# Centring the values inside the RWKV-7 recurrence, and splitting the squares of its output into a rounded and a low part

## The chip, the cores and the metric

One core of one Trainium2 chip runs the whole program in one launch. The time is device microseconds (us) from launch to end, the median of several executions; lower is better. Engine names in the profile: PE is TensorE's matmul, PEld its weight load, DVE is VectorE, ACT is ScalarE, POOL is GpSimd, SP is SyncE, which issues most transfers.

## The reference, cut to what matters

The model is two layers of a block with three branches (RWKV-7, retention, a spatial gating unit), each followed by a gated feed-forward part, and then a second block with attention and experts. The change lies in the RWKV-7 branch, whose output is normalised per head of 64 features:

```python
def rwkv7_scan(r, w, k, v, kk, a):
    def step(state, inp):
        sa = jnp.einsum('bhvk,bhk->bhv', state, -kk_t)
        state = (state * w_t[:, :, None, :] + sa[..., None] * (kk_t * a_t)[:, :, None, :]
                 + v_t[..., None] * k_t[:, :, None, :])
        y = jnp.einsum('bhvk,bhk->bhv', state, r_t)
        return state, y
...
y = rwkv7_scan(r, decay, k, v, kk, a)                       # (1, 512, 8, 64)
mean = jnp.mean(y, axis=-1, keepdims=True)
var = jnp.mean(jnp.square(y - mean), axis=-1, keepdims=True)
y = (y - mean) * lax.rsqrt(var + RW_GN_EPS) * lnx_g + lnx_b
y = y + jnp.sum(r * k * r_k, axis=-1, keepdims=True) * v
```

The output y is linear in v, and the feature index over which the mean is taken is v's own. A v from which the mean over its 64 features was taken therefore gives a y whose mean over them is zero. The bonus term at the end uses v itself, uncentred.

## The kernel before

Activations lie with features on the 128 partitions and 512 tokens along the row: a 1024 wide activation is eight tiles of 128x512, the RWKV-7 output y four (`PAIRS`, two heads of 64 in a tile). Large products are made in three passes: the weights and the activations are split into a rounded part in the type fp32r and a low part (what rounding left), and hi·hi, hi·lo and lo·hi are added up in one PSUM bank. The weights' rounded part is made by ACT (`high`, L1309) and their low part by POOL (`low`, L1437); the low part of an activation is made by DVE. Products whose operands are plain f32 are not split; the trace shows two PE instructions for each of those.

`back_phase` runs once for each of the two layers. Its first part is 24 tiles, i = 0 to 23 (`gate_and_branch(i)`): a gate product of depth 8 (L1485, L1489, L1494), then a branch product of depth 4 (L1505, L1514, L1520), for the retention branch in tiles 0 to 7, the gating unit in 8 to 15 and RWKV-7 in 16 to 23. Between the passes of tiles 0 to 10, `beneath(slot)` places the recurrence itself: chunks of 64 tokens, worked on by small 64x64 f32 matmuls (L960, L1075, L1087). Each engine has its own program, written out by hand in the order of issue, and the engines wait for each other on semaphores that count up.

What the change touches, by engine:

- PE. In three of the recurrence's turns (`TURNS`, through `by_features`, L956 to L960) beta, value and kappa are turned from features-by-tokens to tokens-by-features by a matmul against the identity. Behind tile 10, `means()` (L1525 to L1529) sums y over each head with four matmuls against a block matrix of ones (`head_ones`); behind tile 11, `variances()` (L1531) does the same for the squares; behind tile 12, `out_gates()` (L1541) makes four more products.
- DVE. `recurrence_vector` (L1200) begins with a copy of the chunks' decay (L1203). It is issued behind `begin_x` (L990) and `low_y(RET, 0)` (L1774, four subtractions), and ahead of the first mask (L1242), which empties the PSUM bank that PE's next slot writes to. `centre()` (L1777, its instruction is L1780) subtracts the mean from y behind tile 10, in place.
- ACT. In tile 11, behind the gate's sigmoid, `squares()` (L1665) squares the centred y into `sq`; `logs()` and `roots()` turn the variances into factors.
- POOL. `low(n)` for the gate and the branch of each tile, 128x1024 and 128x512, and one mask of the recurrence (`next_bt`, L996) for each level.

In each tile POOL's `low` follows ACT's `high`, and ACT's follows the last pass of PE's product before.

Of the kernel before, what the change touches and what calls it, by code (L numbers as in the profile page):

```python
# [17 lines left out]
F32 = mybir.dt.float32  # L18
F32R = mybir.dt.float32r
ALU = mybir.AluOpType  # L20
# [3 lines left out]
P = 128  # L24
# [882 lines left out]
class Recurrence:  # L907
# [4 lines left out]
    def __init__(self, nc, T, home, R):  # L912
        U = self.U
        in_x = iter(range(KD))
        in_w = iter(range(6))
        in_runs = iter((60, 62, 64, 66))

        def x(_):
            return T.xT[:, next(in_x), :].rearrange("p (u c) -> p u c", u=U)

        def w(_):
            i = next(in_w)
            return T.w[:, 0, i * S:i * S + S].rearrange("p (u c) -> p u c", u=U)

        def runs(n):
            return over(nc, home + next(in_runs) * 1024, "rec_" + n, U, C)

        self.LT, self.X, self.T1, self.BT = x("LT"), x("X"), x("T1"), x("BT")
        self.bT, self.kT, self.vT = (x("bT0"), w("bT1")), (x("kT0"), w("kT1")), (x("vT0"), w("vT1"))
        self.XT, self.AkT = (x("XT0"), runs("XT1")), (w("AkT0"), runs("AkT1"))  # L930
        self.AbrT, self.AkrT = (w("AbrT0"), runs("AbrT1")), (w("AkrT0"), runs("AkrT1"))
        self.M, self.Rs, self.Un = (over(nc, home + kb * 1024, "rec_" + n, PAIRS, C)
                                    for kb, n in ((69, "M"), (48, "Rs"), (49, "Un")))
        self.decay = over(nc, home + 68 * 1024 + 512, "rec_decay", PAIRS, NCH)
        self.masks, self.alpha, self.beta, self.rho, self.kappa = R.masks, R.alpha, R.beta, R.rho, R.kappa
        self.value, self.y = R.p[:, 8:12, :], R.y

# [18 lines left out]
def by_features(nc, T, Q, g, bank, lhs, rhs, u, h):  # L956

    half, j, now = HEAD_HALVES[h], u % PAIRS, chunk_tokens(2 * g + u // PAIRS)
    rhs = T.ident[half, half] if rhs is None else rhs[half, j, now]
    return nc.tensor.matmul(bank[token_half(h), u * C:u * C + C], lhs[half, j, now], rhs, start=True, stop=True)  # L960


# [36 lines left out]
def recurrence_tensor(nc, T, pe, q, Q):  # L999
# [19 lines left out]
    def wait_fill(g, t):  # L1019
        if t == KEY_SUM:  # L1020
            pe.wait_ge(q["lt_ready"], g + 1)
        elif t == BETA_TURN:
            pe.wait_ge(q["masked"], 3 * g + 1)
        elif t == BETA_SUM:
            pe.wait_ge(q["turned_taken"], 3 * g + 1)
        elif t == VALUE_TURN:
            pe.wait_ge(q["masked"], 3 * g + 2)
        elif t == KAPPA_TURN:
            pe.wait_ge(q["turned_taken"], 3 * g + 2)
        elif t == KAPPA_SUM:  # L1030
            pe.wait_ge(q["turned_taken"], 3 * g + 3)
        elif t == NEXT_L:
            pe.wait_ge(q["masked"], 3 * g + 3)
# [166 lines left out]
def recurrence_vector(nc, T, dve, q, Q, R):  # L1200

    link = Chain(dve, q["clock"])
    link(nc.vector.tensor_copy(Q.decay[:, :, :], R.runs[:, :, :, C:C + 1].rearrange("p j n a -> p j (n a)")))  # L1203

    def change_state(n):
        dve.wait_ge(q["change_done"], n + 1)
# [10 lines left out]
    def beneath(slot):  # L1217
# [34 lines left out]
        if changing:  # L1252
# [3 lines left out]

REC_SEMS = ("operands_ready product turned turned_taken t1_done t1_taken lt_ready bt_ready masked x_ready xt_begun xt_ready "
            "step_done zeroed right_begun change_begun right_done right_taken y_begun u_done u_taken y_part change_done "
            "changed state_ready y_done y_taken clock")


BACK_SEMS = ("m_full*2 x_full w_full*2 w_hi w_lo done clock loaded mean_done centred squared var_done rooted gate_done out_done "
             "y_hi y_lo sig_done added m_hi m_lo x_added x_squared sq_added x_summed norm_rooted "
             "sg_gated u_hi u_lo scaled taps_loaded gate_taken val_taken conv_done silu_done made gains_made z_hi z_lo")
BACK_ORDER = (1, 2, 0)
# [74 lines left out]
class BackWork:  # L1340


    def __init__(self, nc, T, home):
        def at(skip, name, *shape, dt=F32):
            return over(nc, home + int(skip * 1024), "back_" + name, *shape, dt=dt)

        self.y_hi = (at(16, "y_hi_ret", 4, S, dt=F32R), at(106, "y_hi_sg", 4, S, dt=F32R),
                     at(52, "y_hi_rw", 4, S, dt=F32R))
        self.y_lo = (at(0, "y_lo_ret", 4, S, dt=F32R), at(8, "y_lo_sg", 4, S, dt=F32R),
                     at(40, "y_lo_rw", 4, S, dt=F32R))  # L1350
        self.merged, self.m_lo = at(86, "merged", KD, S), at(86, "m_lo", KD, S, dt=F32R)
        self.sq, self.rstd, self.up = at(24, "sq", PAIRS, S), at(32, "rstd", PAIRS, S), at(70, "up", RW_W)
        self.w_hi, self.w_lo = T.next_hi, T.w_lo
        self.m_hi, self.sig = at(0, "m_hi", KD, S, dt=F32R), at(102, "sig", 2, S)

        self.made_hi, self.made_lo = at(0, "made_hi", FT, S, dt=F32R), at(44, "made_lo", FT, S, dt=F32R)
        self.sq_sum, self.x_rstd = at(102, "sq_sum", S), at(104, "x_rstd", S)
        self.un, self.x_sq = at(106, "un", 4, S), at(106, "x_sq", 2, S)
        self.conv, self.taps = at(88, "conv", 4, S), at(132, "taps", FT, 8)
        self.next_sq = at(106, "next_sq", 2, S)  # L1360


def back_phase(nc, T, f, q, stale, layer, R, y_ret, y_sg, B, Q, late, gain):
# [33 lines left out]
    with nc.Block() as block:  # L1397
# [59 lines left out]
        def _(pe):  # L1457
# [64 lines left out]
                mm.then_inc(f["done"], 1)  # L1522
                beneath(next(slots))

            def means():  # L1525
                pe.wait_ge(q["y_taken"], NCH)
                for j in range(PAIRS):
                    nc.tensor.matmul(T.ps[4 + j][:, :], T.head_ones[:, :], y_rw[:, j, :], start=True,
                                     stop=True).then_inc(f["mean_done"], 1)  # L1529

            def variances():  # L1531
                for j in range(PAIRS):
                    pe.wait_ge(f["squared"], j + 1)
                    nc.tensor.matmul(T.ps[4 + j][:, :], T.head_ones[:, :], B.sq[:, j, :], start=True,
                                     stop=True).then_inc(f["var_done"], 1)

            def out_gates():
# [80 lines left out]

            for i in range(24):
                gate_and_branch(i)  # L1620
                if i == 10:
                    means()
                if i == 11:
                    variances()
                if i == 12:
                    out_gates()
# [20 lines left out]
        def _(act):  # L1647
# [12 lines left out]
                    nc.scalar.copy(B.y_hi[part][:, k, :], y[part][:, k, :]).then_inc(f["y_hi"], 1)  # L1660

            def squares():
                for j in range(PAIRS):
                    act.wait_ge(f["centred"], j + 1)
                    nc.scalar.activation(B.sq[:, j, :], y_rw[:, j, :], ACT.Square).then_inc(f["squared"], 1)  # L1665

            def logs():

# [99 lines left out]
        def _(dve):  # L1768
# [5 lines left out]
                    nc.vector.tensor_tensor(B.y_lo[part][:, k, :], y[part][:, k, :], B.y_hi[part][:, k, :].bitcast(F32),  # L1774
                                            ALU.subtract).then_inc(f["y_lo"], 1)

            def centre():  # L1777
                for j in range(PAIRS):
                    dve.wait_ge(f["mean_done"], j + 1)
                    nc.vector.scalar_tensor_tensor(out=y_rw[:, j, :], in0=T.ps[4 + j][:, :], scalar=-1.0 / 64,  # L1780
                                                   in1=y_rw[:, j, :], op0=ALU.mult, op1=ALU.add).then_inc(
                                                       f["centred"], 1)

            def finish_out(j):

# [81 lines left out]
            for i in range(24):  # L1867
# [6 lines left out]
                if i == 5:  # L1874
                    low_y(SG, 4)
                if i == 10:
                    centre()
                if i in (13, 14):
                    finish_out(2 * i - 26)
                    finish_out(2 * i - 25)  # L1880
# [2085 lines left out]
```

## Time and profile before

| what | value |
|---|---|
| median of 3 runs (lowest to highest) | 2836.72 us (2835.44 to 2837.39) |
| span of the profiled execution, first to last instruction | 2839.8 us |
| PE busy | 2777.4 us, 98% |
| DVE, ACT, POOL busy | 1445.8, 1099.1, 1080.0 us: 51%, 39%, 38% |
| granted TensorE clock, mean | 0.994 |
| transfers | 413.83 MB, 146 GB/s on average |

The profile is one execution, and its span is 3.1 us (0.1%) longer than the median of the runs; the runs themselves lie within 2 us. A busy share says little of a single stretch. In a stretch where PE has no gap, what leaves PE shortens the program, and what leaves another engine doesn't. Where PE has a gap, the question is what ended it. In the views, times are from the start of the span; the last bracket of a timeline row is the idle time ahead of it and the instruction that released it. The first layer's back phase starts at about 254 us, the second's at about 1176 us.

### The profile page before, as it was taken

What the parts mean: (1) busy time and instruction counts of PE and PEld (TensorE: products, weight loads), DVE (VectorE), ACT (ScalarE), POOL (GpSimd) and SP (SyncE); (2) the same over time, 40 slices, a digit from 0 to 9 for tenths busy, and PEclk for the clock granted to TensorE, in tenths of its full rate; (3) what the DMA queues carried; (4) which work ended last, traced back from release to release, by engine and by line L of the source; (5) the groups of instructions that cost most, each with busy time, mean ns of one, the idle gap of its engine ahead of it and who ended that gap; (6) DMA issues with size and microseconds to landing.
All of it is one profiled execution on the core that took longest, in us unless ns stands there. A gap on an engine that the chain in (4) does not pass through costs nothing. (4 is left out here: it accounts for less than half of the span.)

```text
span 2839.8 us, 45477 instructions
## 1 busy us (share of the span) xinstructions
PE 2777.4 (98%) x18996; PEld 2064.6 (73%) x18997; DVE 1445.8 (51%) x1776; ACT 1099.1 (39%) x1613; POOL 1080.0 (38%) x627
## 2 busy tenths in 40 slices
PE   8999999999999999999999999999999989999997
PEld 6777777888888877777888888877778764445543
DVE  6267434578862526743457785269855232222223
ACT  4484324343332448433434333255575331111112
POOL 4365433444444436543444444434444221211110
PEclk9999999999999999999999999999999999999999
DMA  5222122222222422212222232232222149999995
GB/s 178 75 86 72 48 106 89 83 92 102 94 107 96 164 71 86 72 48 106 89 87 100 89 104 96 97 107 84 88 79 104 48 189 387 419 414 413 411 411 235
DMA packets 63070, 413.83 MB, mean 146 GB/s; under 512 B 9504, under 2 KB 10272, under 8 KB 25632
## 3 DMA queue, kind: packets, MB, share of 16 engines
q1 hardware_dynamic: 62880, 411.11, 38.4%
q8 instruction: 142, 2.33, 0.3%
q14 instruction: 48, 0.39, 0.0%
HBM read 401.64 MB, written 4.19 MB: 143 GB/s over the span
## 5 line engine op out<-in xcount | busy, mean ns | idle before, releaser
L1437 POOL TENSOR_TENSOR w_lo<-w,next_hi 128x1024 fp32r<-128x1024 f32 (+1 forms) x244 | 546.3, 2243 | 644.9 <-ACT next_hi L1656 433.9
L1656 ACT CAST next_hi<-w 128x1024 fp32r<-128x1024 f32 (+1 forms) x152 | 156.0, 1026 | 268.7 <-PE bank L1468 249.3
L312 POOL TENSOR_TENSOR w_lo<-w,next_hi 128x1024 fp32r<-128x1024 f32 x64 | 162.3, 2537 | 223.5 <-ACT next_hi L510 223.5
L3506 PE MATMUL bank<-moe_w,moe_hg 128*64 128x512 f32 x1024 | 225.8, 594 | 0.0
L2291 POOL TENSOR_TENSOR mid_w_lo<-w,mid_w_hi 128x1024 fp32r<-128x1024 f32 x60 | 149.2, 2490 | 183.8 <-ACT mid_w_hi L2753 183.4
L3506 PEld LDWEIGHTS bank<-moe_w,moe_hg 128*64 128x64 f32 x1024 | 73.4, 137 | 141.1 <-issue 141.1
L1463 PE MATMUL bank<-h_hi,next_hi 128*128 128x512 f32 x688 | 171.1, 391 | 1.5 <-DVE back_made_lo L1861 1.5
L1465 PE MATMUL bank<-h_lo,next_hi 128*128 128x512 f32 x688 | 169.9, 389 | 0.0
L1468 PE MATMUL bank<-h_hi,w_lo 128*128 128x512 f32 x688 | 169.9, 389 | 0.0
L1748 ACT ACTIVATE back_conv<-back_un,back_taps 128x512 f32<-128x512 f32 x88 | 71.8, 816 | 238.8 <-DVE back_un L1845 238.8
L1309 ACT CAST next_hi<-w 128x1024 fp32r<-128x1024 f32 x96 | 80.1, 835 | 213.3 <-PE bank L1494 157.4
L1463 PEld LDWEIGHTS bank<-h_hi,next_hi 128*128 128x128 f32 x688 | 129.0, 188 | 29.9 <-DVE back_made_lo L1861 2.3
L1465 PEld LDWEIGHTS bank<-h_lo,next_hi 128*128 128x128 f32 x688 | 129.2, 188 | 26.8
L1468 PEld LDWEIGHTS bank<-h_hi,w_lo 128*128 128x128 f32 x688 | 129.2, 188 | 26.8
L1849 DVE SCALAR_TENSOR_TENSOR back_conv<-back_un,back_taps,back_conv 128x511 f32<-128x511 f32 x88 | 90.2, 1026 | 86.6 <-ACT back_conv L1748 86.6
L3447 POOL COPY moe_quad_place<-moe_place 128x16 f32 (+1 forms) x7 | 1.4, 198 | 347.7 <-PE bank L3560 347.7
L510 ACT CAST next_hi<-w 128x1024 fp32r<-128x1024 f32 x64 | 66.9, 1045 | 130.0 <-PE bank L392 69.0
L3574 PE MATMUL bank<-moe_w,moe_midT 128*64 128x512 f32 x512 | 113.3, 595 | 2.6 <-ACT moe_midT L3650 2.6
L1860 DVE CAST back_made_hi<-back_conv 128x512 fp32r<-128x512 f32 x44 | 109.6, 2491 | 1.5
L1827 DVE TENSOR_TENSOR xT<-xT,bank 128x512 f32<-128x512 f32 x32 | 22.0, 688 | 172.1 <-PE bank L1468 170.1
L1812 DVE TENSOR_TENSOR back_sig<-back_sig,bank 128x512 f32<-128x512 f32 x32 | 22.0, 688 | 171.0 <-PE bank L1520 131.7
L3697 DVE TENSOR_TENSOR xT<-xT,bank 128x512 f32<-128x512 f32 x120 | 74.3, 681 | 65.0 <-PE bank L3520 65.0
(620 smaller groups left out, 6478.4 us busy)
## 6 DMA issues: line engine op xcount, KB each, us to landing
moe_w<-in_moe_w SPq DMA_DIRECT2D x128, 1024.0 KB, 13.1
moe_w<-in_moe_w SPq DMA_DIRECT2D x32, 2048.0 KB, 12.3
w<-in_ffn_up SPq DMA_DIRECT2D x44, 1024.0 KB, 4.8
w<-in_w_merge SPq DMA_DIRECT2D x48, 768.0 KB, 4.3
w<-in_w_in SPq DMA_DIRECT2D x30, 1024.0 KB, 4.9
w<-in_w_mid SPq DMA_DIRECT2D x29, 1024.0 KB, 4.8
w<-in_ffn_down SPq DMA_DIRECT2D x16, 1408.0 KB, 5.8
w<-in_w_out SPq DMA_DIRECT2D x16, 512.0 KB, 4.4
```

Of the source, the lines that this page charges most:

```text
L312: nc.gpsimd.tensor_tensor(split(w_lo, c, t), raw(c, t), split(w_hi, c, t).bitcast(F32), ALU.subtract).then_inc(f["w_lo"], 1)
L1309: nc.scalar.copy(w_hi[:, n % 2, 0:merge_depth(n), :], merge_raw(T, n)).then_inc(f["w_hi"], 1)
L1437: nc.gpsimd.tensor_tensor(split(B.w_lo, n), raw(n), split(B.w_hi, n).bitcast(F32), ALU.subtract).then_inc(f["w_lo"], 1)
L1463: nc.tensor.matmul(bank, B.w_hi[:, n % 2, k, :], x_hi[:, cols], start=start and k == 0, stop=False)
L1465: nc.tensor.matmul(bank, B.w_hi[:, n % 2, k, :], x_lo[:, cols], start=False, stop=False)
L1468: mm = nc.tensor.matmul(bank, B.w_lo[:, n % 2, k, :], x_hi[:, cols], start=False, stop=stop and k == len(hi) - 1)
L1656: nc.scalar.copy(split(B.w_hi, n), raw(n)).then_inc(f["w_hi"], 1)
L1849: link(nc.vector.scalar_tensor_tensor(out=c[:, 1:S], in0=u[:, 0:S - 1], scalar=tap(1), in1=c[:, 1:S], op0=ALU.mult, op1=ALU.add))
L1860: link(nc.vector.tensor_copy(hi, product))
L2291: nc.gpsimd.tensor_tensor(split(B.w_lo, n), raw(n), split(B.w_hi, n).bitcast(F32), ALU.subtract).then_inc(f["w_lo"], 1)
L3506: mm = nc.tensor.matmul(bank[half_of(u), :], hg[:, k, slots_of(b, u)], w[:, u, k * 512:k * 512 + 512], start=(k == 0), stop=(k == KD - 1))
L3574: mm = nc.tensor.matmul(y_banks[half][half_of(u), :], midT[:, f, half_of(u)], w2[:, u, c:c + 512], start=(f == 0), stop=(f == 3))
```

## The change

Three edits, in each of the two layers.

1. The recurrence gets values that are already centred. A 64x64 matrix, the identity less 1/64 everywhere (`Q.centre`, once for each half of the partitions), is made by two DVE instructions at the start of the recurrence and takes the identity's place when the values are turned. PE waits for the two (semaphore `centre_made`) ahead of that turn.
2. `means()` on PE and `centre()` on DVE go, with their semaphores.
3. ACT rounds the ones to fp32r (`sum_heads`) and squares y straight into an fp32r tile (`sq_hi`). DVE makes the whole squares in f32 (`sq`) and subtracts the rounded ones (`sq_lo`). The sum over a head is one fp32r product of the rounded part and one of the low part, where there was one f32 product.

```diff
 def by_features(nc, T, Q, g, bank, lhs, rhs, u, h):
-    rhs = T.ident[half, half] if rhs is None else rhs[half, j, now]
+    if rhs is None:
+        rhs = Q.centre[half, :] if lhs is Q.value else T.ident[half, half]
+    else:
+        rhs = rhs[half, j, now]
...
         elif t == VALUE_TURN:
+            pe.wait_ge(q["centre_made"], 2)
             pe.wait_ge(q["masked"], 3 * g + 2)
...
     link(nc.vector.tensor_copy(Q.decay[:, :, :], ...))
+    for half in HEAD_HALVES:
+        nc.vector.scalar_tensor_tensor(out=Q.centre[half, :], in0=T.head_ones[half, half], scalar=-1.0 / C,
+                                       in1=T.ident[half, half], op0=ALU.mult, op1=ALU.add).then_inc(q["centre_made"], 1)
...
-            def means():
-                pe.wait_ge(q["y_taken"], NCH)
-                for j in range(PAIRS):
-                    nc.tensor.matmul(T.ps[4 + j][:, :], T.head_ones[:, :], y_rw[:, j, :], start=True,
-                                     stop=True).then_inc(f["mean_done"], 1)
-
             def variances():
                 for j in range(PAIRS):
                     pe.wait_ge(f["squared"], j + 1)
-                    nc.tensor.matmul(T.ps[4 + j][:, :], T.head_ones[:, :], B.sq[:, j, :], start=True,
+                    nc.tensor.matmul(T.ps[4 + j][:, :], B.sum_heads[:, :], B.sq_hi[:, j, :], start=True, stop=False)
+                    pe.wait_ge(f["sq_split"], j + 1)
+                    nc.tensor.matmul(T.ps[4 + j][:, :], B.sum_heads[:, :], B.sq_lo[:, j, :], start=False,
                                      stop=True).then_inc(f["var_done"], 1)
...
             def squares():
+                act.wait_ge(q["y_taken"], NCH)
+                nc.scalar.copy(B.sum_heads[:, :], T.head_ones[:, :])
                 for j in range(PAIRS):
-                    act.wait_ge(f["centred"], j + 1)
-                    nc.scalar.activation(B.sq[:, j, :], y_rw[:, j, :], ACT.Square).then_inc(f["squared"], 1)
+                    nc.scalar.activation(B.sq_hi[:, j, :], y_rw[:, j, :], ACT.Square).then_inc(f["squared"], 1)
...
-            def centre():
+            def split_squares():
+
+                dve.wait_ge(q["y_taken"], NCH)
                 for j in range(PAIRS):
-                    dve.wait_ge(f["mean_done"], j + 1)
-                    nc.vector.scalar_tensor_tensor(out=y_rw[:, j, :], in0=T.ps[4 + j][:, :], scalar=-1.0 / 64,
-                                                   in1=y_rw[:, j, :], op0=ALU.mult, op1=ALU.add).then_inc(
-                                                       f["centred"], 1)
+                    nc.vector.tensor_tensor(B.sq[:, j, :], y_rw[:, j, :], y_rw[:, j, :], ALU.mult).then_inc(
+                        f["sq_whole"], 1)
+                for j in range(PAIRS):
+                    dve.wait_ge(f["sq_whole"], j + 1)
+                    dve.wait_ge(f["squared"], j + 1)
+                    nc.vector.tensor_tensor(B.sq_lo[:, j, :], B.sq[:, j, :], B.sq_hi[:, j, :].bitcast(F32),
+                                            ALU.subtract).then_inc(f["sq_split"], 1)
```

DVE at the start of the first layer's recurrence, before. `back_y_lo_ret` is the low part of the retention branch's output, `w` the tile that the first mask fills:

```order
118 L1774 TENSOR_TENSOR back_y_lo_ret_215<-y_ret,back_y_hi_ret_209 128x512 x4
119 L1203 COPY rec_decay_267<-rw_runs 128x32
120 L1242 TENSOR_TENSOR w<-bank,rw_masks_207 128x512
121 L1810 TENSOR_TENSOR back_merged_221<-back_sig_233,bank 128x512
122 L1226 TENSOR_TENSOR xT<-xT,bank 128x512
```

The same place in the changed program:

```order
119 L1208 COPY rec_decay_273<-rw_runs 128x32
120 L1210 SCALAR_TENSOR_TENSOR rec_centre_275<-head_ones,ident 64x64 x2
121 L1250 TENSOR_TENSOR w<-bank,rw_masks_207 128x512
122 L1820 TENSOR_TENSOR back_merged_221<-back_sig_239,bank 128x512
123 L1234 TENSOR_TENSOR xT<-xT,bank 128x512
```

Two instructions now stand between the copy of the decay and the first mask; both read two tiles in SBUF.

PE at the ends of tiles 10 and 11, before (the 64x64 work is over by then):

```order
1644 L1520 MATMUL bank<-back_y_hi_sg_211,w_lo_57 128x512 x4
1645 L1528 MATMUL bank<-rw_p,head_ones 128x512 x4
1646 L1485 MATMUL bank<-h_hi_50,next_hi_55 128x512 x8
1647 L1489 MATMUL bank<-h_lo,next_hi_55 128x512 x8
1648 L1494 MATMUL bank<-h_hi_50,w_lo_57 128x512 x8
1649 L1505 MATMUL bank<-back_y_hi_sg_211,next_hi_55 128x512 x4
1650 L1514 MATMUL bank<-back_y_lo_sg_217,next_hi_55 128x512 x4
1651 L1520 MATMUL bank<-back_y_hi_sg_211,w_lo_57 128x512 x4
1652 L1534 MATMUL bank<-back_sq_225,head_ones 128x512 x4
1653 L1485 MATMUL bank<-h_hi_50,next_hi_55 128x512 x8
```

And in the changed program, from the end of tile 11:

```order
1650 L1530 MATMUL bank<-back_y_hi_sg_211,w_lo_57 128x512 x4
1651 L1538 MATMUL bank<-back_sq_hi_225,back_sum_heads_229 128x512
1652 L1540 MATMUL bank<-back_sq_lo_227,back_sum_heads_229 128x512
1653 L1538 MATMUL bank<-back_sq_hi_225,back_sum_heads_229 128x512
1654 L1540 MATMUL bank<-back_sq_lo_227,back_sum_heads_229 128x512
1655 L1538 MATMUL bank<-back_sq_hi_225,back_sum_heads_229 128x512
1656 L1540 MATMUL bank<-back_sq_lo_227,back_sum_heads_229 128x512
1657 L1538 MATMUL bank<-back_sq_hi_225,back_sum_heads_229 128x512
1658 L1540 MATMUL bank<-back_sq_lo_227,back_sum_heads_229 128x512
1659 L1495 MATMUL bank<-h_hi_50,next_hi_55 128x512 x8
```

The four f32 products against the ones (L1528) are gone from the end of tile 10, and the four of tile 11 have become eight in fp32r, each of the low ones behind a wait of its own.

DVE at the same tiles, before and then in the changed program:

```order
210 L1812 TENSOR_TENSOR back_sig_233<-back_sig_233,bank 128x512
211 L1817 TENSOR_TENSOR back_merged_221<-back_merged_221,back_sig_233 128x512
212 L1780 SCALAR_TENSOR_TENSOR rw_p<-bank,rw_p 128x512 x4
213 L1812 TENSOR_TENSOR back_sig_233<-back_sig_233,bank 128x512
214 L1817 TENSOR_TENSOR back_merged_221<-back_merged_221,back_sig_233 128x512
```

```order
211 L1822 TENSOR_TENSOR back_sig_239<-back_sig_239,bank 128x512
212 L1827 TENSOR_TENSOR back_merged_221<-back_merged_221,back_sig_239 128x512
213 L1786 TENSOR_TENSOR back_sq_231<-rw_p 128x512 x4
214 L1791 TENSOR_TENSOR back_sq_lo_227<-back_sq_231,back_sq_hi_225 128x512 x4
215 L1822 TENSOR_TENSOR back_sig_239<-back_sig_239,bank 128x512
216 L1827 TENSOR_TENSOR back_merged_221<-back_merged_221,back_sig_239 128x512
```

Four instructions with one input in PSUM have become eight that read SBUF alone, and tile 11's addition to the merged tile stands behind them.

## Rows read from the trace of the kernel before

**Rows 1.** The page: busy us of each engine, share of the span, instructions
```profile
PE 2777.4 (98%) x18996; PEld 2064.6 (73%) x18997; DVE 1445.8 (51%) x1776; ACT 1099.1 (39%) x1613; POOL 1080.0 (38%) x627
```
**Rows 2.** Timeline of PE, tiles 10 to 12: start, us, instructions
```profile
414.17 3.59 PE L1528 MATMUL bank<-rw_p,head_ones 128*128 128x512 f32 x8
417.19 2.39 PE L1485 MATMUL bank<-h_hi,next_hi 128*128 128x512 f32 x8
419.42 1.98 PE L1489 MATMUL bank<-h_lo,next_hi 128*128 128x512 f32 x8
421.24 1.98 PE L1494 MATMUL bank<-h_hi,w_lo 128*128 128x512 f32 x8
...
425.77 3.59 PE L1534 MATMUL bank<-back_sq,head_ones 128*128 128x512 f32 x8
428.80 2.39 PE L1485 MATMUL bank<-h_hi,next_hi 128*128 128x512 f32 x8
```
**Rows 3.** Timeline of ACT, tile 11
```profile
424.69 2.18 ACT L1665 ACTIVATE back_sq<-rw_p 128x512 f32<-128x512 f32 x4
426.77 0.60 ACT L1309 CAST next_hi<-w 128x512 fp32r<-128x512 f32 x1
```
**Rows 4.** Timeline of POOL, tiles 10 and 11
```profile
415.06 1.27 POOL L1437 TENSOR_TENSOR w_lo<-w,next_hi 128x512 fp32r<-128x512 f32 x1 [0.73 <-ACT next_hi L1309]
424.38 2.40 POOL L1437 TENSOR_TENSOR w_lo<-w,next_hi 128x1024 fp32r<-128x1024 f32 x1 [8.06 <-ACT next_hi L1309]
427.46 1.27 POOL L1437 TENSOR_TENSOR w_lo<-w,next_hi 128x512 fp32r<-128x512 f32 x1 [0.67 <-ACT next_hi L1309]
```
**Rows 5.** Timeline of DVE, tiles 10 and 15
```profile
415.16 1.71 DVE L1817 TENSOR_TENSOR back_merged<-back_merged,back_sig 128x512 f32<-128x512 f32 x1
...
468.05 2.48 DVE L1774 TENSOR_TENSOR back_y_lo_rw<-rw_p,back_y_hi_rw 128x512 fp32r<-128x512 f32 x4
```
**Rows 6.** Timelines of DVE and POOL late in the first layer's front stage
```profile
242.68 1.66 DVE L784 TENSOR_TENSOR rw_beta<-rw_alpha,front_a 128x512 f32<-128x512 f32 x1
...
242.05 3.44 POOL L342 TENSOR_TENSOR y_sg<-front_sg_tmp,y_sg 128x512 f32<-128x512 f32 x2
```
**Rows 7.** Timelines of DVE and POOL, start of the first recurrence
```profile
258.28 2.38 DVE L1203 COPY rec_decay<-rw_runs 128x32 f32<-128x32 f32 x1
260.70 0.69 DVE L1242 TENSOR_TENSOR w<-bank,rw_masks 128x512 f32<-128x512 f32 x1
...
257.99 2.63 POOL L1437 TENSOR_TENSOR w_lo<-w,next_hi 128x1024 fp32r<-128x1024 f32 x1 [1.73 <-ACT next_hi L1309]
260.57 1.28 POOL L996 TENSOR_TENSOR xT<-xT,rw_masks 128x512 f32<-128x512 f32 x1
261.80 1.29 POOL L1437 TENSOR_TENSOR w_lo<-w,next_hi 128x512 fp32r<-128x512 f32 x1
```
**Rows 8.** Timeline of PE there, then the second layer's waits
```profile
261.54 0.24 PE L1075 MATMUL bank<-xT 64*64 64x64 f32 x1 [0.68 <-DVE w L1242]
...
PE bank L1075 <- DVE w L1242: 0.6, 1, 0.6
```
**Rows 9.** Timelines of DVE and POOL early in the front stage
```profile
51.04 0.68 DVE L678 TENSOR_TENSOR front_ret_tmp<-front_qk,front_cossin 128x512 f32<-128x512 f32 x1
...
50.71 3.27 POOL L312 TENSOR_TENSOR w_lo<-w,next_hi 128x1024 fp32r<-128x1024 f32 x1 [5.17 <-ACT next_hi L510]
```
**Rows 10.** Timeline of PE, both front stages, first and ninth group of L367
```profile
43.55 0.71 PE L367 MATMUL bank<-next_hi,front_early_hi 128*128 128x256 f32 x4 [2.03 <-DVE front_early_lo_b L820]
...
47.46 0.64 PE L367 MATMUL bank<-w_lo,front_early_hi 128*128 128x256 f32 x4
...
963.39 0.71 PE L367 MATMUL bank<-next_hi,front_early_hi 128*128 128x256 f32 x4 [2.03 <-DVE front_early_lo_b L820]
...
968.78 0.64 PE L367 MATMUL bank<-w_lo,front_early_hi 128*128 128x256 f32 x4
```
**Rows 11.** Window of PE: us, busy (matmuls), granted clock, DMA share, GB/s
```profile
964.60:968.00 3.40, 3.40 (x18) 0.50 1.05 316
```

More of the change, by code:

```diff
@@ L934, in __init__ @@
         self.decay = over(nc, home + 68 * 1024 + 512, "rec_decay", PAIRS, NCH)
+        self.centre = over(nc, home + 68 * 1024 + 128, "rec_centre", C)
         self.masks, self.alpha, self.beta, self.rho, self.kappa = R.masks, R.alpha, R.beta, R.rho, R.kappa
@@ L1258 @@
             "step_done zeroed right_begun change_begun right_done right_taken y_begun u_done u_taken y_part change_done "
-            "changed state_ready y_done y_taken clock")
-BACK_SEMS = ("m_full*2 x_full w_full*2 w_hi w_lo done clock loaded mean_done centred squared var_done rooted gate_done out_done "
+            "changed state_ready y_done y_taken centre_made clock")
+BACK_SEMS = ("m_full*2 x_full w_full*2 w_hi w_lo done clock loaded squared sq_whole sq_split var_done rooted gate_done out_done "
              "y_hi y_lo sig_done added m_hi m_lo x_added x_squared sq_added x_summed norm_rooted "
@@ L1351, in __init__ @@
         self.merged, self.m_lo = at(86, "merged", KD, S), at(86, "m_lo", KD, S, dt=F32R)
+        self.sq_hi, self.sq_lo = at(16, "sq_hi", PAIRS, S, dt=F32R), at(0, "sq_lo", PAIRS, S, dt=F32R)
+        self.sum_heads = at(48, "sum_heads", P, dt=F32R)
         self.sq, self.rstd, self.up = at(24, "sq", PAIRS, S), at(32, "rstd", PAIRS, S), at(70, "up", RW_W)
@@ L1620, in _ @@
                 gate_and_branch(i)
-                if i == 10:
-                    means()
                 if i == 11:
@@ L1876, in _ @@
                 if i == 10:
-                    centre()
+                    split_squares()
                 if i in (13, 14):
```

## The prediction

> **What bounds the kernel now.** I read the page first: PE is busy 98% of the span [rows 1], so what counts is what enters or leaves PE's own stream, and any gap in it. Then the timeline of PE at the two places that the diff touches: at tiles 10 to 12 there is no gap at all, the next product starts where the last leaves off [rows 2]; at the start of the recurrence there is one of 0.68 us, ended by DVE's first mask [rows 8]. Last the timelines of DVE and POOL beside them, since the change gives DVE new work at both places. The same stretches in the second layer read alike, 0.6 us for the gap [rows 8], so each term is worked out in the first and doubled.
>
> What the reader is to see in the rows of DVE and POOL is that some instructions of the two exclude each other. A DVE subtraction of two SBUF tiles of 128x512 takes 0.68 us by itself, 2.48 us for four in a row, so a step of 0.60 [rows 5]. L1817, of the same form, is issued at 415.16 beside a POOL instruction that runs from 415.06 to 416.33 and takes 1.71: it ends 0.54 behind POOL's [rows 4, 5]. Where both have work waiting they alternate: L784 takes 1.66 while POOL's pair L342 takes 3.44 [rows 6], where a 128x512 of POOL takes 1.27 alone [rows 4]. The smallest sees it too: the copy of 32 columns L1203 takes 2.38 and ends with POOL's L1437, at 260.66 [rows 7]. The mask behind it, with one input in PSUM, runs its 0.69 beside a busy POOL undisturbed [rows 7].
>
> **The change part by part, for one layer.**
>
> *Means gone.* The four sums leave PE: 417.19 - 414.17 = 3.02 us. The first pass of the gate behind them steps by 419.42 - 417.19 = 2.23, the next by 421.24 - 419.42 = 1.82 [rows 2]; I put the 0.41 down to the change from f32 to fp32r products, and it goes too. Together -3.43 us. PE did not wait for the last chunk of y there, so nothing takes the place of this work; the weights of tile 11 are ready (POOL's low for it ends at 416.33 [rows 4], and tile 11's branch now comes at 419.6 instead of 423.05). DVE's centring was no wait of PE's.
>
> *Variances.* In PE's stream, 3.03 us (425.77 to 428.80) become eight passes of 1.82/8 = 0.227, which is 1.82 us, and the 0.41 behind them goes: -1.62 us if nobody makes PE wait [rows 2]. But PE takes the low part of each square behind the rounded part, and DVE makes the four low parts only now. In the clock of the old trace (tile 11 as a whole moves, its parts with it): ACT's squares start at 424.69, step by about 0.52, and a copy of the ones goes ahead of them, between nothing and the 0.60 of a 128x512 [rows 3]; for a quarter of the columns I take 0.2. The first rounded square is there at 425.5. POOL holds on until 426.78 [rows 4]. So the first low part ends at 426.78 + 0.54 = 427.3, the second at 427.9. POOL's next, L1437 at 427.46 plus the 0.2 [rows 4], comes in behind the second by the alternation of [rows 6] and runs from 427.8 to 429.1; the third low part ends at 429.6, the fourth at 430.25. A semaphore's 0.1 and a last pass of 0.23, and the gate of tile 12 starts at 430.6 where it started at 428.80: +1.8 - 0.41 = +1.39 us. The other end, with no exclusion: low parts at 426.2, then a step of 0.60 to 428.0, the gate at 428.4, which is -0.8 us. I take +1.39, because form, engines and neighbours are those of the rows. The four whole squares on DVE are free: they follow L1817 at 416.9, end at 419.3, and POOL's next comes at 424.38 - 3.43 = 420.95. ACT's logarithms now end at about 431.3, and the products that need the roots come a tile later, behind 5.4 us of gate and 2.7 of branch: no wait. DVE's addition for tile 11 waits behind the low parts until about 431.7; PE asks for it two tiles on.
>
> *The centring matrix.* Two DVE instructions on 64x64 are put ahead of the mask that ended PE's gap [rows 7, 8]. Both have two SBUF inputs. The first is issued at 260.7, when POOL's L996 is already running, and can't go before 261.85. POOL's next, L1437 at 261.80 [rows 7], is then waiting already; by alternation it takes its turn between the two and holds until 263.1. The second matrix half ends at 263.25, and the mask starts at 263.17 instead of 260.70: PE goes on 2.47 us later. Lower end: unhindered, at most 0.2 each, +0.4. Middle: the second slips in behind the first, mask at about 262.05, +1.35. I take +2.47. Nothing behind gives it back, since PE has next to no other gap in the recurrence. The turn itself costs the same with either matrix, and the wait for `centre_made` is behind the mask's in DVE's order, so it costs nothing.
>
> The Trainium skill ("SBUF — State Buffer", "Who interferes with whom") says that whoever issues first gets the shared pair of ports for the whole instruction and the other fully blocks; by that, POOL's L1437, issued at 261.80, goes ahead of the second matrix half, and the term is +2.47. One row speaks against it: POOL's L312 is issued at 50.71 and takes 3.27, longer than its usual 2.40 by more than one DVE instruction has left, and DVE's L678, issued after it at 51.04, runs its plain 0.68 [rows 9]; so POOL was passed once. By that row the term would be +1.35. The sum by the rule is 2.2 us above the sum by the row, over two layers.
>
> *The granted clock.* PE's gap at the start of the recurrence grows from 0.68 to 3.15 us, and at the variances it now stands for 1.45 and again for 1.2 us within 4.4. In the second layer a gap of 2.03 us ahead of 963.39 is followed by a stretch at 0.50, 1.2 instead of 2.4 GHz, with 18 passes in 3.4 us [rows 11]; in the first layer the same gap of 2.03 ahead of 43.55 is not. The ninth group of passes comes 5.39 us after the first in the one and 3.91 in the other [rows 10]: a fall costs 1.48 us. So 2.03 us of idleness is about even. I give 3.15 us a chance of 0.8 in each layer, the broken gap at the variances 0.45: my estimates. That is 2 x 0.8 x 1.48 = 2.4 and 2 x 0.45 x 1.48 = 1.3 us.
>
> *Sum.* 2 x (-3.43 + 1.39 + 2.47) = +0.9, and 3.7 for the clock: +4.6 us. The profiled execution spans 2839.8 us, 3.1 more than the median of the runs; the terms are differences within it, so I put them on the median, 2836.7 + 4.6 = 2841.3 us.
>
> **The rivals.** A measurement of this kernel can tell about 0.2% from no change, 5.7 us: faster is below 2831.0, slower above 2842.4.
>
> (a) DVE is hardly held up at the matrix: both halves run before POOL's L996 takes hold, or are too short to matter. For it: the copy of 32 columns slipped out within 0.05 us of POOL's end [rows 7]. Against: it had waited 2.3 us first. 2 x (-3.43 + 1.39 + 0.4) = -3.3, with the clock's 1.3 at the variances 2834.7.
>
> (b) One wait at the matrix, not two, as [rows 9] has it: 2 x (-3.43 + 1.39 + 1.35) = -1.4, with a gap of 2.03 us that is even for the clock (1.5) and 1.3 at the variances: 2838.1.
>
> (c) DVE keeps clear of POOL at both places, by an order of arrival other than mine: 2 x (-3.43 - 0.8 + 0.4) = -7.7, 2829.0 us; with no wait at all at the variances 2827.4. For it speaks only what the PE stream sheds; against it every row of 4 to 7.
>
> (d) The slower side: TensorE's clock falls at all four of the new gaps. Mechanism: idleness of PE at the matrix and at the variances, in both layers, each followed by 3.4 us at 0.50. It costs 4 x 1.48 = 5.9, and with the 0.9 it is 2843.5 us. It decides from the fourth fall on: three give 2842.0, which is still within the bound. For it: at the matrix the gap is half as long again as the one that was followed by a fall. Against: two shorter gaps with work between them at the variances, and a gap of 2.03 that went without.
>
> **How the numbers follow.** The forecast, both waits and two or three falls of the clock (0.9 to 5.3 us above, 2837.6 to 2842.5), 0.55; (a) 0.10; (b) 0.12; (c) 0.11; (d) 0.12. Faster comes from (c) with a trace of (a), 0.12; slower from (d) and the top of the forecast's own spread, 0.20; the rest, 0.68, is no change that can be told. The range leaves out (c) and what lies beyond (d): 2832.5 to 2844.5. The time is the forecast's 2841.3.
>
> **What would show it.** No instruction of the sums behind tile 10, and tile 11's gate right behind tile 10's branch, first pass in 1.8. At the matrix: the two 64x64 instructions with durations of about 1.2 and 1.3 us rather than 0.2, each ending with a POOL instruction; PE's gap ahead of L1075's successor near 3.1 us, released by the mask. At tile 11: low parts of squares that end in two pairs, 427.3 and 427.9, then 429.6 and 430.2 relative to a gate that ends where it did, with PE's waits put down to them. The granted clock at 0.50 for some 3.4 us behind the first of these. I am wrong if the small instructions take 0.2 us beside a running POOL; if POOL's low and DVE's low part of a square overlap; if the first pass after tile 10 still takes 2.2; or if PE's gap grows and the clock stays at 1.00 in both layers, which alone takes the time down by some 2 to 4 us.

## The result, and the profile after

The changed kernel is slightly slower: 2842.58 us against 2838.66 us in the same session, a ratio of 1.0014 with a 95% interval of [1.0008, 1.002] over 21 executions of each. That is +3.9 us, where +4.6 was forecast. (The kernel before was 2836.72 us in its first three runs and between 2838.66 and 2839.47 later, so from here on each time is given as its ratio to the kernel before in the same session; a square bracket is the 95% interval. One of the 21 executions of the kernel before took 6938.8 us; the median hardly feels it.)

DVE, then POOL, at the start of the first recurrence in the changed kernel; they answer to [rows 7]. The columns are start, us, instructions.

```profile
257.09 2.38 DVE L1208 COPY rec_decay<-rw_runs 128x32 f32<-128x32 f32 x1
259.50 2.44 DVE L1210 SCALAR_TENSOR_TENSOR rec_centre<-head_ones,ident 64x64 f32<-64x64 f32 x2
261.98 0.69 DVE L1250 TENSOR_TENSOR w<-bank,rw_masks 128x512 f32<-128x512 f32 x1
...
256.79 2.63 POOL L1447 TENSOR_TENSOR w_lo<-w,next_hi 128x1024 fp32r<-128x1024 f32 x1 [1.73 <-ACT next_hi L1317]
259.38 1.27 POOL L1000 TENSOR_TENSOR xT<-xT,rw_masks 128x512 f32<-128x512 f32 x1
260.61 1.26 POOL L1447 TENSOR_TENSOR w_lo<-w,next_hi 128x512 fp32r<-128x512 f32 x1
```

The two 64x64 instructions take 2.44 us together. By themselves they take 1.22 and 1.19 us and end at 260.72 and 261.95, each some 0.08 us behind a POOL instruction (L1000 ends at 260.65, L1447 at 261.86): one wait for each. What PE waited for, in the first layer and then in the second, answers to [rows 8] (engine and line, what it waited for, us in total, times, longest):

```profile
PE bank L1080 <- DVE w L1250: 3.2, 1, 3.2
PE bank L1540 <- DVE back_sq_lo L1791: 2.2, 2, 1.2
...
PE bank L1080 <- DVE w L1250: 3.1, 1, 3.1
PE bank L1540 <- DVE back_sq_lo L1791: 2.2, 2, 1.2
```

The gap of 0.7 has become 3.2, and the variances have brought two new ones. PE at tiles 11 and 12, with [rows 2] for the kernel before, then DVE and POOL there, with [rows 4, 5]:

```profile
416.77 1.98 PE L1495 MATMUL bank<-h_hi,next_hi 128*128 128x512 f32 x8
418.58 1.98 PE L1499 MATMUL bank<-h_lo,next_hi 128*128 128x512 f32 x8
...
424.93 0.39 PE L1538 MATMUL bank<-back_sq_hi,back_sum_heads 128*128 128x512 f32 x1
426.53 0.50 PE L1540 MATMUL bank<-back_sq_lo,back_sum_heads 128*128 128x512 f32 x1 [1.22 <-DVE back_sq_lo L1791]
...
428.82 0.50 PE L1540 MATMUL bank<-back_sq_lo,back_sum_heads 128*128 128x512 f32 x1 [0.95 <-DVE back_sq_lo L1791]
...
429.76 2.00 PE L1495 MATMUL bank<-h_hi,next_hi 128*128 128x512 f32 x8
...
424.77 4.60 DVE L1791 TENSOR_TENSOR back_sq_lo<-back_sq,back_sq_hi 128x512 fp32r<-128x512 f32 x4 [2.87 <-ACT back_sq_hi L1670]
...
423.54 2.39 POOL L1447 TENSOR_TENSOR w_lo<-w,next_hi 128x1024 fp32r<-128x1024 f32 x1 [4.59 <-ACT next_hi L1317]
426.82 1.40 POOL L1447 TENSOR_TENSOR w_lo<-w,next_hi 128x512 fp32r<-128x512 f32 x1 [0.89 <-ACT next_hi L1317]
```

The gate's first pass steps by 1.81 where it stepped by 2.23, so the 0.41 us behind the means is gone with them. The four low parts take 4.60 us, where four such instructions in a row take 2.48 [rows 5], and the sums occupy PE from 424.93 to 429.76, 4.83 us for the 3.03 of before. One by one the low parts end at 426.48, 427.08, 428.77 and 429.37: two pairs, with a POOL instruction ahead of each. The granted clock behind the new gaps, in windows of PE (us, busy and matmuls, clock, DMA share, GB/s), with [rows 11] for the pattern:

```profile
264.00:267.40 3.40, 3.40 (x12) 0.54 0.35 142
1185.60:1189.00 3.40, 3.05 (x67) 0.54 0.67 233
...
425.00:429.70 4.70, 2.53 (x9) 1.00 0.68 255
```

It fell behind the matrix in both layers and did not fall at the variances.

From the third pass of tile 0's gate (L1504, L1494 in the kernel before) to the gate of tile 12, the first layer takes 429.76 - 253.53 = 176.2 us where it took 174.1, and the second 175.5 where it took 173.3: +4.4 us for both. The two profiled spans differ by 3.0 us only, because the changed kernel's execution reached the first of these places 1.2 us sooner, before anything that the change touches, and that although its clock had fallen once in the first front stage (window 42.20:45.50, 0.53), where the other execution's had not.

### The profile page after: what moved, and what is told of

It reads as the page before. It is cut to its first block and busy times, and to the rows that moved or that the text cites. A ratio compares the mean times of both kernels' runs of the same rounds, so it can differ in the third digit from the quotient of the medians.

```text
span 2842.8 us, 45475 instructions
## 1 busy us (share of the span) xinstructions
PE 2773.0 (98%) x18980; PEld 2064.7 (73%) x18981; DVE 1457.8 (51%) x1788; ACT 1099.3 (39%) x1615; POOL 1080.1 (38%) x627
## 5 line engine op out<-in xcount | busy, mean ns | idle before, releaser
L1447 POOL TENSOR_TENSOR w_lo<-w,next_hi 128x1024 fp32r<-128x1024 f32 (+1 forms) x244 | 546.8, 2245 | 640.6 <-ACT next_hi L1660 433.7
L3642 ACT ACTIVATE moe_silu<-bank,moe_slot_gate 128x512 f32<-128x512 f32 x16 | 11.0, 688 | 240.7 <-PE bank L3516 240.7
```

Of the source, the lines that this page charges most:

```text
L1447: nc.gpsimd.tensor_tensor(split(B.w_lo, n), raw(n), split(B.w_hi, n).bitcast(F32), ALU.subtract).then_inc(f["w_lo"], 1)
```

## The experiments

**1. The matrix made later.** DVE makes it behind the second slot's transpose.

```diff
-    for half in HEAD_HALVES:
-        nc.vector.scalar_tensor_tensor(out=Q.centre[half, :], ...)
...
         if changing:
             decay_state(n)
+        if slot == 1:
+            for half in HEAD_HALVES:
+                nc.vector.scalar_tensor_tensor(out=Q.centre[half, :], ...)
```

> The changed kernel with one thing moved: DVE makes the two halves of the centring matrix behind its transpose of the recurrence's second slot, where POOL is idle and PE waits for nothing of DVE's, instead of ahead of the first mask. Theory (the matrix waits twice for POOL ahead of the mask that PE needs, and the gap of 3.1 us then brings the clock down): the two instructions take about 0.2 us each, PE's gap is 0.68 us again, the granted clock stays at 1.00 there, and the time falls by 2 x (2.47 + 1.48) = 7.9 us against the changed kernel, to 0.9986 of the kernel before. Rival (the gap costs its own length but the fall of the clock is made good later by other slack): 4.9 us less, 0.9997. Rival (the loss of the changed kernel lies at the variances, the gap at the matrix is caught up): no difference, 1.0014.

0.9990 of the kernel before, [0.9981, 0.9999]; against the changed kernel's 1.0014 that is 6.8 us less, for 7.9 expected. DVE at the new place, and PE's gap:

```profile
261.64 0.42 DVE L1261 SCALAR_TENSOR_TENSOR rec_centre<-head_ones,ident 64x64 f32<-64x64 f32 x2
...
259.08 0.24 PE L1080 MATMUL bank<-xT 64*64 64x64 f32 x1 [0.69 <-DVE w L1247]
...
259.40:268.00 8.60, 8.60 (x210) 1.00 0.29 97
```

The same two instructions take 0.42 us with POOL idle, the gap is that of before, and the clock stays. The loss at the matrix was a matter of place. The rival of no difference, 1.0014, lies outside the interval. The other rival, a gap without a price for the clock, 0.9997, lies inside it, so the time alone does not exclude it; what the clock costs is read from the traces and experiment 4.

**2. The squares in f32 again.**

```diff
-                    nc.tensor.matmul(T.ps[4 + j][:, :], B.sum_heads[:, :], B.sq_hi[:, j, :], start=True, stop=False)
-                    pe.wait_ge(f["sq_split"], j + 1)
-                    nc.tensor.matmul(T.ps[4 + j][:, :], B.sum_heads[:, :], B.sq_lo[:, j, :], start=False,
+                    nc.tensor.matmul(T.ps[4 + j][:, :], T.head_ones[:, :], B.sq[:, j, :], start=True,
```

> The changed kernel with the third edit undone: ACT squares y in f32, PE sums the squares in one f32 product for each tile, DVE makes no whole squares and no low parts; the centred values stay. Theory (the low parts wait for POOL, twice, and cost PE more than the single passes save): PE has no gap at tile 12's start, the variances take 3.03 us again and 0.41 us is lost behind them, and the time falls by about 2 x (1.0 to 1.4) = 2 to 3 us against the changed kernel, to about 1.0005 of the kernel before. Rival (single passes are worth their 1.2 us even so): 1 to 3 us slower than the changed kernel, 1.002.

0.9999, [0.999, 1.0008]: 4.3 us less than the changed kernel, where 2 to 3 were expected; the interval holds both, and it excludes the rival's 1.002. PE has no gap there, and its rows are those of before:

```profile
425.55 3.59 PE L1538 MATMUL bank<-back_sq,head_ones 128*128 128x512 f32 x8
428.58 2.39 PE L1495 MATMUL bank<-h_hi,next_hi 128*128 128x512 f32 x8
430.81 1.52 PE L1499 MATMUL bank<-h_lo,next_hi 128*128 128x512 f32 x6
```

3.03 us, and the first pass behind steps by 2.23 again. In the trace of the changed kernel the same stretch, sums and first pass behind, takes 6.67 us (424.93 to 431.60) against 5.26 here: as the changed kernel places it, the third edit costs 1.41 us a layer.

**3. Writes without reads in the matrix's place.**

```diff
-        nc.vector.scalar_tensor_tensor(out=Q.centre[half, :], in0=T.head_ones[half, half], ...)
+        nc.vector.memset(Q.centre[half, :], 1.0 / C)
```

> The changed kernel, but the two instructions ahead of the first mask are memsets of the same two tiles to a constant: nothing is read from SBUF. It leaves the centring out, so that the values are multiplied by a constant matrix. Theory (what costs is the second SBUF input, which DVE can't read while POOL reads): each takes 0.1 to 0.2 us beside a busy POOL, PE's gap is about 1.0 us instead of 3.1, the clock doesn't fall there; against the changed kernel 2 x (2.1 + 1.48) = 7 us less, 0.9990 of the kernel before. Rival (any DVE instruction waits there, since a third in the row has to wait for POOL in any form): gap and time as in the changed kernel.

The time, 1.0602, says nothing of this place, and the expected 0.9990 stays unanswered: the extra time of some 167 us against the changed kernel lies behind 2.8 ms, where PE runs more products of the experts (1152 of L3515's against 1024 of them in the changed kernel; their number depends on the data). The stretch itself can be read, DVE, then POOL, then PE's wait:

```profile
257.18 2.38 DVE L1208 COPY rec_decay<-rw_runs 128x32 f32<-128x32 f32 x1
259.63 0.29 DVE L1210 MEMSET rec_centre<- 64x64 f32 x2
259.96 0.69 DVE L1249 TENSOR_TENSOR w<-bank,rw_masks 128x512 f32<-128x512 f32 x1
...
259.47 1.27 POOL L1000 TENSOR_TENSOR xT<-xT,rw_masks 128x512 f32<-128x512 f32 x1
...
PE bank L1080 <- DVE w L1249: 1.0, 1, 1.0
```

At the same place, beside the same POOL instruction, two memsets take 0.29 us where the two instructions that read two SBUF tiles take 2.44. The rival, that a third DVE instruction in a row waits in any form, falls. What the experiment compares is no input with two, though. Of one input in SBUF the rows have two cases: the mask, whose other input is in PSUM, runs 0.69 us beside POOL, and the decay's copy, whose only input is in SBUF, waits like the two matrix instructions.

**4. PE kept busy in the gap.**

```diff
                 mm.then_inc(f["done"], 1)
+                if i == 0:
+                    for _ in range(3):
+                        nc.tensor.matmul(T.ps[2][:, :], T.head_ones[:, :], R.p[:, 13, :], start=True, stop=True,
+                                         skip_group_check=True)
                 beneath(next(slots))
```

> The changed kernel with three more f32 products of 128x512 on PE, in the gap at the start of the recurrence, into a bank that the next tile begins afresh: 3 x 0.76 = 2.3 us of work that nobody needs, ahead of the matmul that waits for the mask. Theory (the gap ends when the mask does, whatever PE did in it, and idleness of 3.1 us brings the clock down): the waiting matmul starts at the same time, its gap is about 0.9 us, the clock stays at 1.00 behind it, and the time falls by 2 x 1.48 = 3.0 us against the changed kernel, to 1.0004 of the kernel before, in spite of more work. Rival (the clock's fall comes of something else, such as the 64x64 products that follow): the clock falls all the same, no difference or up to 1 us slower than the changed kernel.

1.0009, [1.0, 1.0018], 1.4 us less than the changed kernel, for 3.0 expected; the intervals overlap, so the time says no more than that 2.3 us of added work in each layer cost nothing. The trace says the rest: PE's gap is 0.61 us, and its clock behind it 1.00, in both layers.

```profile
PE bank L1080 <- DVE w L1250: 0.6, 1, 0.6
...
262.00:266.00 4.00, 3.97 (x128) 1.00 0.56 201
```

So it was idleness that brought the clock down, not what came after: the same small products follow in both kernels, and without the long idle stretch there was no fall in two layers, with it one in each. This profiled execution had a fall at the variances instead (from 426.7 us), and at 316 us, in the recurrence, PE stood for 1.1 us without a cause that the profile shows.

**5 and 7. PE's sums one tile later**, with the matrix moved (5), and with nothing else (7).

```diff
-                if i == 11:
+                if i == 12:
                     variances()
-                if i == 12:
+                if i == 13:
                     out_gates()
...
-                if i in (13, 14):
-                    finish_out(2 * i - 26)
-                    finish_out(2 * i - 25)
+                if i in (14, 15):
+                    finish_out(2 * i - 28)
+                    finish_out(2 * i - 27)
```

> The changed kernel with both places mended: the centring matrix made behind the second slot as in the first experiment, and PE's sums of squares behind tile 12 instead of tile 11 (logarithms and roots in tile 13, the end of the normalisation in tiles 14 and 15, each one tile later; the squares and their low parts are made where they were). Theory: no gap at either place, and the two gains stand alone, 2 x (-3.43 - 1.62) = -10.1 us, 0.9964 of the kernel before. Rival (the normalised y is now late for tile 16's branch): a gap of PE ahead of tile 16's branch of some us in each layer, 0.998 to 1.000.

> The changed kernel with PE's sums of squares one tile later and nothing else: the matrix stays ahead of the mask. Theory: PE's gaps at the variances (1.22 and 0.95 us) go, the eight passes take 1.82 us and nothing behind them is slowed; the gap of 3.1 us at the matrix stays with its fall of the clock. 2 x (1.62 + 1.0 to 1.4) = 4 to 6 us less than the changed kernel counting that the passes' own 1.2 us then show, that is about 4.5 us, 0.9998 of the kernel before. Rival (the gaps at the variances cost nothing because PE would wait there anyhow): no difference from the changed kernel, 1.0014.

0.9997, [0.9988, 1.0006], and 1.0028, [1.0016, 1.0039]. The theory's 0.9964 and 0.9998 were both missed, and the rival that was named for 5 came true. PE at tile 16 and then its clock, in 5:

```profile
461.97 1.98 PE L1505 MATMUL bank<-h_hi,w_lo 128*128 128x512 f32 x8
466.29 1.98 PE L1516 MATMUL bank<-back_y_hi_rw,next_hi 128*128 128x512 f32 x4 [2.35 <-ACT back_y_hi_rw L1665]
468.10 1.75 PE L1525 MATMUL bank<-back_y_lo_rw,next_hi 128*128 128x512 f32 x4
...
468.50:471.90 3.40, 3.40 (x10) 0.53 0.00 0
```

The gaps at the variances are gone and one of 2.35 us stands ahead of tile 16's branch, with a fall of the clock behind it in each layer of both kernels. 2 x (2.35 + 1.48) = 7.7 us, 0.0027, takes 0.9964 to 0.9991 and 0.9998 to 1.0025, each within the measured interval. The chain from the variances to the normalised y had less than a tile of slack, which I had not checked.

**6. The copy of the decay moved too.**

```diff
-    link(nc.vector.tensor_copy(Q.decay[:, :, :], ...))
...
         if slot == 1:
+            link(nc.vector.tensor_copy(Q.decay[:, :, :], ...))
```

> As the kernel with both places mended, and the copy of the chunks' decay is moved behind the second slot too, out of the way of the first mask. Theory (the 0.68 us that PE waited there in the kernel before is the same wait of DVE's copy for POOL): the mask starts right behind the low parts of the retention output, about 2.3 us earlier, PE has no gap there, and 2 x 0.68 = 1.4 us more go: 0.9959 of the kernel before. Rival (the mask then waits for something else, the product or a semaphore): the gap stays near 0.6 us and the time is that of the kernel without this move.

0.9989, [0.998, 0.9998]; 0.9959 was missed, since this kernel has 5's gap at tile 16 as well. The move itself is to be read against 5: 2.3 us less, for 1.4 expected, which the overlapping intervals do not tell from nothing. The rows do: PE's gap at the first mask is gone altogether. DVE there, in experiment 9's kernel, which has the same order at this place:

```profile
256.54 0.68 DVE L1246 TENSOR_TENSOR w<-bank,rw_masks 128x512 f32<-128x512 f32 x1
...
261.60 0.15 DVE L1259 COPY rec_decay<-rw_runs 128x32 f32<-128x32 f32 x1
```

The copy that took 2.38 us beside POOL's instruction takes 0.15 with POOL idle.

**8 and 11. The first two edits alone**, with the matrix moved (8), and the copy as well (11); the third edit undone as in experiment 2.

> The first two edits alone, with the matrix out of the way: centred values, no means, matrix behind the second slot, squares summed in one f32 product as before. Theory: the gain is that of the means alone, 2 x 3.43 = 6.9 us, 0.9976 of the kernel before, and the kernel with both places mended is 3.2 us faster than this one. Rival (single passes for the squares gain nothing even with their waits hidden): this one is as fast as the kernel with both places mended.

> The first two edits alone with the matrix and the decay's copy both behind the second slot: centred values, no means, squares summed in f32 as before. Theory: the gain of the means and of the gap of 0.68 us that the kernel before had, 2 x (3.43 + 0.68) = 8.2 us, 0.9971 of the kernel before; 0.0005 less than with the copy left where it was.

0.9976, [0.9967, 0.9985], and 0.9971, [0.9961, 0.9982]: both on the expected figure. The first is 6.8 us below the kernel before, for the means' computed 6.9; the second is 1.4 us less again, the old gap, which is less than the intervals can tell apart. The other half of 8's theory was missed: the kernel with both places mended (5, 0.9997) is 6 us slower than this one, not 3.2 us faster. It had the wait at tile 16, so this says nothing of the single passes; 9 answers that.

**9. The rounded squares made one tile earlier**, with the matrix and the decay's copy moved as in 6, and PE's sums left behind tile 11.

```diff
                 high(2 * i + 3)
                 beneath(next(slots))
+                if i == 10:
+                    squares()
...
-                if i == 11:
-                    squares()
```

> The changed kernel with the matrix and the decay's copy behind the second slot, and ACT's rounded squares made at the end of tile 10 instead of in tile 11, so that DVE can make the low parts before POOL's next instruction; PE's sums stay behind tile 11. Theory: DVE's low parts start at once behind its whole squares, two or three of the four are done when POOL starts, the last ends within 0.5 us of PE's need; PE has at most one gap of 0.3 us there. 2 x (-3.43 - 1.62 + 0.2 - 0.68) = -11 us, 0.9961 of the kernel before. Rival (the low parts still meet POOL's 128x1024 and end as late as in the changed kernel): the gaps at the variances stay near 1 us each, 0.997 to 0.998.

0.9959, [0.9945, 0.9973], for 0.9961 expected: 11.6 us less than the kernel before by the ratio (five executions), and the fastest of all. DVE, POOL and PE there:

```profile
413.87 2.48 DVE L1787 TENSOR_TENSOR back_sq<-rw_p 128x512 f32<-128x512 f32 x4
416.28 2.49 DVE L1792 TENSOR_TENSOR back_sq_lo<-back_sq,back_sq_hi 128x512 fp32r<-128x512 f32 x4
...
417.97 4.78 POOL L1448 TENSOR_TENSOR w_lo<-w,next_hi 128x1024 fp32r<-128x1024 f32 x2 [4.57 <-ACT next_hi L1318]
...
419.35 0.39 PE L1539 MATMUL bank<-back_sq_hi,back_sum_heads 128*128 128x512 f32 x1
419.58 0.39 PE L1541 MATMUL bank<-back_sq_lo,back_sum_heads 128*128 128x512 f32 x1
...
421.17 1.98 PE L1496 MATMUL bank<-h_hi,next_hi 128*128 128x512 f32 x8
```

The low parts run undisturbed and this time POOL waits: its pair takes 4.78 us where 2.40 and 1.27 would do. PE's sums take 421.17 - 419.35 = 1.82 us, with no gap. Here the single passes are worth 0.9971 - 0.9959 = 0.0012, 3.4 us, against the 3.2 of 2 x 1.62; the intervals overlap, but PE's rows show it: 1.82 us and no gap, with 1.81 for the first pass behind.

**10. The end of the normalisation in one tile**, on top of experiment 6.

```diff
-                if i in (14, 15):
-                    finish_out(2 * i - 28)
-                    finish_out(2 * i - 27)
+                if i == 14:
+                    for j in range(PAIRS):
+                        finish_out(j)
```

> The kernel with both places mended and the copy moved, with one more change: DVE finishes the normalised y in tile 14 alone (four tiles of y in a row), not in tiles 14 and 15. Theory (the 2.35 us that PE waited ahead of the branch of tile 16 came of the end of the normalisation moved one tile back): that gap goes, and the time falls by 2 x (2.35 + up to 1.48) = 4.7 to 7.7 us against the kernel with the copy moved, to 0.9965 of the kernel before, give or take 0.0005. Rival (DVE's additions for tile 15 are now late and PE or ACT waits for them): a new gap in tile 16 or 17 of 1 to 2 us, 0.998.

0.9979, [0.997, 0.9988], 2.8 us less than experiment 6, not 4.7 to 7.7, and the intervals overlap. The gap ahead of tile 16's branch shrinks to 1.35 us and doesn't go. DVE, then POOL:

```profile
457.64 2.60 DVE L1799 SCALAR_TENSOR_TENSOR rw_p<-rw_p,layer_cols,back_rstd 128x512 f32<-128x512 f32 x1
460.27 1.67 DVE L1801 SCALAR_TENSOR_TENSOR rw_p<-rw_p,layer_cols,rw_bonus 128x512 f32<-128x512 f32 x1
...
457.29 4.10 POOL L1448 TENSOR_TENSOR w_lo<-w,next_hi 128x1024 fp32r<-128x1024 f32 x2 [4.46 <-ACT next_hi L1318]
```

Two of the twelve instructions, 0.75 us each elsewhere, met POOL's pair: 2.8 us lost to the very exclusion that the document is about. I had counted them at their plain durations. The clock did not fall behind the gap of 1.35 us in either layer.

## Why the prediction was right

*The means, -3.43 us a layer.* Right. PE goes from tile 10 into tile 11 without a gap, and the first pass steps by 1.81; experiment 8 gives 6.8 us for both layers, where 6.9 was computed.

*The variances, +1.39.* Right: the first layer has (4.83 + 1.84) - (3.03 + 2.23) = +1.41. The pattern was the one described, low parts in two pairs. In detail the two gaps are shorter than I had them, 1.22 and 0.95 us for 1.45 and 1.2. With the eight passes' 1.82 us they make 3.99 of the 4.83; the other 0.84 lies in short stretches between the passes, where I had left some 0.4. The nearness of the total is in part luck.

*The matrix, +2.47.* Right: 3.16 - 0.68 = 2.48. Each instruction paid for one of POOL's. In the working one end doesn't meet the next: the second half was to end at 263.25 and the mask behind it to start at 263.17; by the step of 0.04 that [rows 7] has between copy and mask it is 263.29, and the term +2.59. The row that spoke for a DVE instruction passing a waiting POOL [rows 9] found no second case here, and rivals (a) and (b) fall, (c) as well.

By the rule of the Trainium skill ("SBUF — State Buffer", "Who interferes with whom") whoever issues first has the shared ports, and the trace agrees at this place: POOL's L1447 starts at 260.61 and the second matrix half at 260.76, and it is alike in the second layer. The Trainium skill words the blocking for a whole instruction of DVE's two-port modes; of an instruction with two inputs in SBUF it says that it contends with a GpSimd instruction that reads SBUF.

*The clock, +3.7.* The mechanism was right and the chances were off in both directions. The gap of 3.1 us stands in three profiled kernels (changed, 2 and 7), in two layers each: six falls in six, where I gave 0.8. The gaps at the variances stand in four (changed, 1, 3 and 4): two falls in eight, where I gave 0.45. By these shares, of few cases, the term is 2 x 1.48 + 2 x 0.25 x 1.48 = 3.7, the same sum as mine, by luck. Rival (d), four falls, did not occur in the profiled execution; its odds of one in sixteen by these shares are about half of what I gave it. The forecast's own spread was also misstated: "0.9 to 5.3 us above" is none to three falls and ends at 2842.0, not 2842.5; two or three falls are 3.9 to 5.3.

*The sum.* 0.9 from the three measured terms and 3.0 from the two falls seen is +3.9, and the medians of 21 executions give +3.9. That they meet so closely is chance: the two stretches in the profiles give +4.4, of which 0.5 us is in none of the terms. What stays open is the absolute time: the median of the kernel before moved from 2836.7 to 2838.7 us between sessions. So the forecast of 2841.3 was 0.7 us too high as a difference and 1.3 us too low as a time, and 2842.6, which the prediction's fixed line of 2842.4 would call slower, is +3.9 against the kernel of its own session, below the 5.7 us that it asked for.

## What to carry to other kernels

Before putting a small DVE instruction ahead of one that TensorE waits for, look at what it reads and at what POOL is doing: here 0.2 us of work cost 1.2 us beside POOL when it read two SBUF tiles, 0.15 us of copying cost 2.4 when it read one and nothing else, and a memset that read none took 0.15 as it was. Work taken off the bounding engine pays only where what replaces it is ready: the same edit was worth +3.9 us in one order and -11.6 us in another that moved the matrix, a copy and the squares. And a gap costs more than its length once the clock follows it.

## What was not expected of the hardware

The granted clock after an idle stretch of a given length is a matter of chance over a part of the range. The gap of 2.0 to 2.1 us in both layers' front stages stands in all thirteen profiled kernels, 26 times; 12 of them were followed by a stretch at 1.2 GHz and 14 were not. After 2.35 us (experiments 5, 6 and 7) it was six in six, after 1.35 (experiment 10) none in two. It fits the spread of single executions, though no run sets it apart: of the changed kernel's 21 the five slowest (2844.6 to 2844.8 us) have a mean clock of 0.992 and the fastest (2839.3) has 0.995.

An f32 product between fp32r products costs TensorE more than its own time: the first pass of eight behind it stepped by 2.23 us instead of 1.82, at full clock in every place of tiles 10 to 13 and every kernel where it stood, and by 1.81 to 1.86 where it was taken out. The runs show the size and not the cause.
